# Scores of the first layer's attention: three products of upper and lower parts for head pairs 1 to 3

## The reference

```python
def _attend(q, k, v):
    s = jnp.einsum('bqkgd,bskd->bkgqs', q, k).astype(jnp.float32) * ATTN_SCALE
    p = jax.nn.softmax(s, axis=-1).astype(v.dtype)
    return jnp.einsum('bkgqs,bskd->bqkgd', p, v)

    o_lat = lax.map(lambda qb: _attend(qb, k_all, v_all), q_blocks)
    y_b = o_lat.swapaxes(0, 1).reshape(B_, S, B_WIDTH) * jax.nn.silu(bz)
```

## Time and profile before

| | |
|---|---|
| median of 3 runs | 1074.33 us (1074.14 to 1074.9) |
| profiled execution | 1075.35 us |
| its span in the trace | 1072.7 us |
| granted TensorE clock | 0.999 |
| PE busy | 1064.1 us (99%), 8092 matmuls |
| DVE busy | 721.6 us (67%) |
| ACT busy | 574.9 us (54%) |
| POOL busy | 141.2 us (13%) |
| first layer's attention, first scores to the last weighing | 193.3 to 267.7 us |

### The profile page before, as it was taken

How to read it: one execution, slowest core, us unless ns; L and a number is a source line. 1 busy time by engine, 2 the same in 40 slices (tenths; PEclk the granted TensorE clock), 3 DMA queues, 4 the chain that set the end, 5 groups by cost and what they waited for, 6 DMA issues and landing times.

```text
span 1072.7 us, 19921 instructions
## 1 busy us (share of the span) xinstructions
PE 1064.1 (99%) x8092; PEld 949.9 (89%) x8092; DVE 721.6 (67%) x1230; ACT 574.9 (54%) x977; POOL 141.2 (13%) x166
## 2 busy tenths in 40 slices
PE   9999999999999999999999999999999999999998
PEld 7887878656898999799999999999998799999997
DVE  5665566387554878778875676666677776766674
ACT  4532676544444567866565554444574555545454
POOL 0000010253200001632531000000023410000000
PEclk9999999999999999999999999999999999999999
DMA  9732121286613442057444364555543334555641
GB/s 382 319 137 66 75 79 40 93 289 213 232 41 119 141 145 80 6 193 236 148 168 158 119 236 161 194 186 170 198 155 103 134 119 153 202 201 177 211 178 39
DMA packets 25386, 168.77 MB, mean 157 GB/s; under 512 B 3280, under 2 KB 3536, under 8 KB 5456
## 3 DMA queue, kind: packets, MB, share of 16 engines
q1 hardware_dynamic: 25152, 167.25, 44.1%
q10 hardware_dynamic: 144, 0.26, 0.1%
HBM read 164.35 MB, written 1.05 MB: 154 GB/s over the span
## 4 chain that ended last, share of the span: by engine, by line
PE 96%; DVE 2%; ACT 2%; issue 0%; DVEq 0%; ACTq 0%
PE bank L437 26%; PE bank L438 25%; PE bank L439 25%; PE bank L1550 2%; PE bank L494 2%; PE bank L1714 2%; PE bank L1704 2%; PE bank L1694 1%; PE bank L1577 1%; PE bank L1568 1%; PE bank L446 1%; PE bank L2363 1%; PE bank L1395 1%; DVE wlo L415 1%; ACT TILE L1753 1%; PE bank L1688 1%
## 5 line engine op out<-in xcount | busy, mean ns | idle before, releaser
L437 PE MATMUL bank<-OPH,whi 128*128 128x256 f32 (+1 forms) x1716 | 519.7, 303 | 0.3
L439 PE MATMUL bank<-OPH,wlo 128*128 128x256 f32 (+1 forms) x1716 | 511.2, 298 | 0.0
L438 PE MATMUL bank<-OPL,whi 128*128 128x256 f32 (+1 forms) x1716 | 511.2, 298 | 0.0
L415 DVE TENSOR_TENSOR wlo<-raw,whi 128x1024 fp32r<-128x1024 f32 (+1 forms) x255 | 304.0, 1234 | 101.4 <-ACT whi L400 101.3
L437 PEld LDWEIGHTS bank<-OPH,whi 128*128 128x128 f32 x1716 | 328.0, 191 | 17.3 <-issue 5.2
L438 PEld LDWEIGHTS bank<-OPL,whi 128*128 128x128 f32 x1716 | 328.2, 191 | 10.0 <-issue 1.2
L439 PEld LDWEIGHTS bank<-OPH,wlo 128*128 128x128 f32 x1716 | 328.0, 191 | 9.8
L400 ACT ACTIVATE whi<-raw 128x1024 fp32r<-128x1024 f32 (+1 forms) x255 | 254.9, 1050 | 74.2 <-PE bank L439 71.9
L437 PE MATMUL bank<-whi,OPH 128*128 128x256 f32 (+2 forms) x272 | 93.8, 345 | 0.2 <-DVE OPL L717 0.2
L438 PE MATMUL bank<-wlo,OPH 128*128 128x256 f32 (+2 forms) x272 | 91.1, 335 | 0.0
L439 PE MATMUL bank<-whi,OPL 128*128 128x256 f32 (+2 forms) x272 | 91.1, 335 | 0.0
(11 more groups left out here) (291 smaller groups left out, 1132.6 us busy)
## 6 DMA issues: line engine op xcount, KB each, us to landing
raw<-in_stream SPq DMA_DIRECT2D x143, 1024.0 KB, 4.9
PROJ<-in_stream SPq DMA_DIRECT2D x5, 1024.0 KB, 18.4
raw<-in_stream SPq DMA_DIRECT2D x4, 1056.0 KB, 8.6
PROJ<-PROJ SPq DMA_DIRECT2D x32, 64.0 KB, 3.9
FIRST<-in_first SPq DMA_DIRECT2D x1, 1248.0 KB, 5.9
C<-in_con SPq DMA_DIRECT2D x1, 1157.5 KB, 7.2
FIRST<-in_first SPq DMA_DIRECT2D x1, 1024.0 KB, 8.0
WST<-in_w_s SPq DMA_DIRECT2D x2, 256.0 KB, 7.3
```

What stands on the lines that cost most here:

```text
L415: nc.vector.tensor_tensor(c.w[1][:, part], c.raw[:, part], c.w[0][:, part].bitcast(F32), ALU.subtract).then_inc(*raises(c.lo[h]))
L437: nc.tensor.matmul(out, w[0], x[0], start=start, stop=False, skip_group_check=skip)
L438: nc.tensor.matmul(out, w[0], x[1], start=False, stop=False, skip_group_check=skip)
L439: return nc.tensor.matmul(out, w[1], x[0], start=False, stop=stop, skip_group_check=skip)
```

## The change

- A new function `part_in_row` splits one 512-wide row into row `row` of OPH (ACT) and OPL (DVE), when its source is ready and the operand's last product (`pr.used`) is done.
- Behind step 2 both key rows of KDUP are split into rows 6 and 7. Behind steps 3, 6 and 10 the queries of pairs 1, 2 and 3 are split into rows 3, 4 and 5, which these pairs' outputs fill only later.
- The scores of pairs 1, 2 and 3 (blocks 4 to 15, six of the eight heads) are three products of these parts, the two heads in turn. Pair 0 keeps its plain products.
- The splits of output rows 6 and 7 move from steps 5 and 6 to steps 17 and 18, and wait for the last scores.

```diff
+            def part_in_row(self, row, src, before, free):
+                st = stage(f"qk{self.l}_row")
+                key = f"scores{self.l}"
+                def act(e):
+                    for point in due(e, before, free):
+                        e.wait_ge(*point)
+                    nc.scalar.activation(OPH[:, row, :], src, ACT.Copy).then_inc(*raises(("y_hi_made", key, row)))
+                def dve(e):
+                    for point in due(e, before, free, ("y_hi_made", key, row)):
+                        e.wait_ge(*point)
+                    nc.vector.tensor_tensor(OPL[:, row, :], src, OPH[:, row, :].bitcast(F32),
+                                            ALU.subtract).then_inc(*raises(("y_lo_made", key, row)))
+                st.act, st.dve = act, dve
+                return ("y_lo_made", key, row)
...
+                if p in self.apart:
+                    for point in due(e, self.apart[p]):
+                        e.wait_ge(*point)
+                    for n, (q, k) in enumerate(((OPH, OPH), (OPH, OPL), (OPL, OPH))):
+                        for r, h, rows in self.heads(j):
+                            mm = nc.tensor.matmul(self.S[j][r].mem[:, 0:nkb * P], q[rows, 2 + p, c0:c0 + P],
+                                                  k[rows, 6 + h // 4, kb0 * P:(kb0 + nkb) * P], start=n == 0, stop=n == 2)
                             if n == 2:
                                 mm.then_inc(*raises(self.S[j][r].full))
                     return
...
-                between = {0: lambda: job("co_0"), 1: lambda: job("co_1"), 2: mo.join_gates}
+                def query_part(p):
+                    at.apart[p] = [*key_parts, hn.part_in_row(2 + p, proj(QB + p)[:, 0, :], hn.q_ready[p], pr.used)]
+
+                def key_part(kv):
+                    key_parts.append(hn.part_in_row(6 + kv, KDUP[:, kv, :], hn.k_ready, pr.used))
+
+                key_parts = []
+                between = {0: lambda: job("co_0"), 1: lambda: job("co_1"),
+                           2: lambda: (mo.join_gates(), key_part(0), key_part(1)), 3: lambda: query_part(1),
+                           6: lambda: query_part(2), 10: lambda: query_part(3)}
...
-            split_at = {2: (0,), 3: (1,), 5: (6,), 6: (7,)} if l == 0 else {3: (0,), 4: (1,), 11: (6, 7)}
+            split_at = {2: (0,), 3: (1,), 17: (6,), 18: (7,)} if l == 0 else {3: (0,), 4: (1,), 11: (6, 7)}
...
+            if l == 0:
+                for k in (6, 7):
+                    y_keys[k] += [u.full for u in at.S[-1]]
```

More of the change, by code:

```diff
@@ L1660, in __init__ @@
                 self.S, self.E, self.T, self.O, self.full = [], [], [], [], []
+                self.apart = {}
             def take_step(self, j):
@@ L1689, in scores @@
                                                   k[rows, keys, SEQ:T], start=n == 0, stop=n == 2)
+                            if n == 2:
+                                mm.then_inc(*raises(self.S[j][r].full))
+                    return
+                if p in self.apart:
[5 more added lines that the diff above has]
+                                                  k[rows, 6 + h // 4, kb0 * P:(kb0 + nkb) * P], start=n == 0, stop=n == 2)
                             if n == 2:
```

## The result

The changed kernel takes 1078.97 us (median of 6, 1076.59 to 1079.7) against 1074.62 us before (median of 6): ratio 1.0038, 95% interval 1.0025 to 1.0051. It is 4.35 us slower, where 1.5 us were forecast; the time lies over the range. The profiled execution took 1079.7 us, with a span of 1077.9 us.

A forecast was written before the change was run, and what follows sets the result against it. PE's queue, busy 1064.1 of 1072.7 us, was taken as the bound: -1.38 (scores) - 0.12 (step 7) + 2.7 (scores of block 4) + 0.3 (row 5) = +1.5 us, median 1075.8 us, range 1073.1 to 1077.8 us.

The forecast's parts named there:

- The wait of block 4: Scores of block 4: PE waits 2.7 us for pair 1's lower query part, delayed through the DVE and ACT queues.
- The lower query part's surcharge: Pair 1's lower split on DVE beside POOL's gate multiplications: 0 to 0.84 us added to block 4's wait, 0.28 taken.
- The products: Scores of blocks 4 to 15 on PE: 0.90 us saved in six wide blocks, 0.48 in six narrow, 1.38 together.
- rival B: Narrow blocks: two heads' weight loads don't fit under 256 columns, each block takes 0.91 us; +3.7 us, 1078.0 us, chance 0.10.
- rows 5: Profile rows of PE's weight loads: one lasts 183 ns, a pair is busy 0.19 us together, read as loads running at once.
- Query parts of pairs 2 and 3 at nothing: Made behind steps 6 and 10, needed at 8 and 12: lateness covered, priced at nothing, else up to 0.56 us each.
- rival C: POOL holds up lower query parts, 0.56 us more at step 3, and blocks 8 and 12 wait: +3.2 us, 1077.5, chance 0.12.
- The 0.12 us before block 7: Scores of block 7: 0.12 us gained because the split of output row 6 leaves step 5.
- The moved splits at steps 17 and 18: End of attention: row 7's lower split delays row 5's, so PE waits 0.3 us there, bound 0 to 0.6 us.
- Rival A: Block 4's wait is hidden, DVE and ACT making the parts in their gaps: -1.2 us, 1073.1 us, chance 0.12.
- No other new wait above 0.5 us: Sign in the changed profile: besides block 4's wait of about 2.7 us, PE gets no new wait over 0.5 us.
- the 0.68 us row that the prediction counted against the exclusion: DVE split of 0.68 us, started while POOL worked; read as not showing that DVE with two SBUF inputs and POOL exclude each other.

The follow-up runs named there:

- experiment 1: Changed kernel with nine dummy float32 matmuls on PE ahead of block 4's wait for its parts: 1076.9 us, ratio 1.0019 to the kernel before.
- experiment 8: Changed kernel with POOL's two gate multiplications behind step 3 instead of 2, the DVE gates behind steps 5 and 6: 1077.98 us, ratio 1.0028 to before.
- experiment 6: Changed kernel with the parts spread over steps 1, 2, 5, 6 and 10, output splits at 7, 9, 11 and 17: 1074.7 us, ratio 1.0 to before.
- experiment 7: The kernel with spread parts (experiment 6), all parts made and waited for, but scores as plain float32 products: 1076.11 us.
- experiment 2: Changed kernel with all parts made and waited for, but scores of pairs 1 to 3 as plain float32 products: 1080.05 us.
- experiment 4: Changed kernel with output row 7 split at step 17 together with row 6, instead of step 18: 1078.62 us.
- experiment 5: Changed kernel with three products for pairs 2 and 3 only, key part behind step 5, row 6 split at 9, row 7 at 17: 1075.4 us, ratio 1.0006.
- experiment 3: Changed kernel with pair 1's query part made behind step 2, right after the key parts, instead of step 3: 1074.59 us, ratio 0.9997 to before.
- experiment 9: Changed kernel with key row 0 at step 1's end, key row 1 and pair 1's query behind 2, output splits at 9, 11, 13, 17: 1074.15 us, ratio 0.9994.
- experiment 10: Changed kernel with three products for pairs 2 and 3 only, key part behind step 2, output splits at 3, 9, 11, 17: 1073.23 us, ratio 0.9985.

## Why the prediction was wrong

**What bounds the kernel**, right: PE's queue. The waits of PE in this stage stand in the final time.

**The wait of block 4**, right in place and cause, near in size: 2.7 us forecast, 2.88 measured. The queues of ACT and DVE ran as followed. In the changed kernel's timelines of DVE (lower key parts, maxima of block 3, lower query part) and ACT (turned copy, upper query part):

```profile
212.16 1.31 DVE L1495 TENSOR_TENSOR OPL<-KDUP,OPH 128x512 fp32r<-128x512 f32 x2 [1.37 <-ACT OPH L1490]
...
214.29 0.75 DVE L1772 TENSOR_REDUCE STAT<-bank 128x1 f32<-128x256 f32 x2
...
216.80 1.34 DVE L1495 TENSOR_TENSOR OPL<-PROJ,OPH 128x512 fp32r<-128x512 f32 x1 [1.11 <-ACT OPH L1490]
...
215.65 0.60 ACT L1243 ACTIVATE TILE<-bank 128x512 f32<-128x512 f32 x1
216.13 0.64 ACT L1490 ACTIVATE OPH<-PROJ 128x512 fp32r<-128x512 f32 x1
```

The maxima come 1.9 us late against the trace of before with its offset of 0.2 us (2.16 forecast; the earlier trace rows). The lower query part's surcharge was 0.66 us, where I had taken 0.28 of a bound of 0 to 0.84. The two misses, 0.26 us too much and 0.38 us too little, nearly cancel, and that the size came out so near is partly luck.

**The step that failed** is the price of the wait: it stands in the sum as "2.7 (scores of block 4)", as if waiting cost PE what it lasts and nothing else. A stretch in which PE idles for 2.2 or 2.9 us has a second price, the low clock in what follows: 2.7 us in the profiled execution, about 2.1 us in the medians (1078.97 - 1076.9, experiment 1). I read the granted clock of the kernel before, 0.999 and a 9 in every slice (90% or more), and did not ask what kept it there: in that trace PE's longest wait is the 1.1 us for line 446 at the very start, which the changed kernel's list above has as well, and in this stage it waits 0.7 us in three pieces. The profile of before could not give the price, but a stretch of idling longer than any in it should have had a term of its own. There was a hint in the kernel itself: it already has a function `keep_clock` (line 441) that gives PE dummy matmuls of ones, called at lines 644 and 651, and experiment 1 uses it for the wait.

The Trainium skill ("TensorE: Matmul & The Clock Gate", Part 1: The HAM clock gate) says that an idle PE goes back to half rate. The traces agree, with 0.50 and 0.57 in the stretches behind an unfilled wait (the changed kernel, experiment 8) and 1.00 behind the filled one of experiment 1. The idle gaps that the page warns of are longer than the 2.9 and 2.2 us that were enough here; the measurement decides.

With that term the sum is 1.5 + 2.7 = 4.2 us, against the 4.45 us of the trace up to the end of the second layer. In the medians the clock is worth 2.1 us, and 3.6 of the 4.35 us are accounted for. Of the rest, experiment 1's trace has 0.4 us at the two late places.

**The products**, right in the price of a block and too high in the sum: 1.38 us forecast. The 1.41 us between the medians of experiments 6 and 7 look like a hit, but their traces have 1.02 us, and those of the changed kernel and experiment 2, the clock set aside, 1.14 us. A narrow block, in PE's timeline of the changed kernel, takes 232.65 - 232.09 = 0.56 us for the forecast 0.55, a wide one 0.89 to 0.91 at full clock:

```profile
232.09 0.39 PE L1718 MATMUL bank<-OPH 64*128 64x256 f32 x2
232.31 0.29 PE L1718 MATMUL bank<-OPL,OPH 64*128 64x256 f32 x2
232.43 0.29 PE L1718 MATMUL bank<-OPH,OPL 64*128 64x256 f32 x2
232.65 1.09 PE L1734 MATMUL bank<-FIRST,TILE 128*128 128x128 f32 x8
```

A product of 256 columns costs 0.12 us with its pair of loads, so rival B falls and rows 5 were read rightly. By the rule of the Trainium skill for loads ("TensorE: Matmul & The Clock Gate", section LDWEIGHTS) two in a row would be 0.21 us, an estimate from that page; the pair overlaps, and the measurement decides. What the prediction had wrong is that a shorter narrow block makes the next start earlier. In the changed kernel it does so only at blocks 11 and 15, 0.09 us each against experiment 2; at blocks 6, 7, 10 and 14 the next start comes when it came with the plain products. There the distances behind them grow by as much (the turning in step 6 takes 1.10 us to the next start, 228.87 to 229.97, and 1.02 us where nothing holds it); what holds it in each step I haven't followed. So the 0.48 us that stand in the sum for the six narrow blocks were at most 0.2.

**Query parts of pairs 2 and 3 at nothing**, right within 0.1 us: the profile shows no wait before blocks 8 and 12 of the changed kernel, and rival C falls as a whole, though its contention was there at step 3. **The 0.12 us before block 7**, too small: it is 3.97 us from block 6 to 7 before and 3.77 in the changed kernel and in experiment 2 alike, so none of these 0.20 us is the products'. The reading took the end of the eight weighing matmuls (0.66 us) for the distance to the next start, which is 0.59 us (231.50 to 232.09). Another 0.11 us come before block 8, in experiment 2 too. These 0.31 us for a forecast 0.12 nearly make up for what the narrow blocks didn't give, and that is luck. **The moved splits at steps 17 and 18**, right: 0.3 us, shown by experiment 4. Rival A fell with the wait. "No other new wait above 0.5 us" did not hold in the trace: the 0.60 us for DVE at 502.86 us are one, though not of the change.

**What stays open.** The 0.3 us at the end of the second layer, a wait for POOL, is there in the changed kernel and in experiments 1, 2, 4, 5 and 8. Experiments 3, 6, 7, 9 and 10 don't have it and even gain 0.25 us there on the kernel before, so two kernels with the same work there can lie 0.5 us apart. I haven't found what it hangs on. Experiment 9 is 0.5 us under before in the medians; its trace is 0.8 us ahead at block 15 against block 3, loses 0.5 us behind it and gains 0.25 us at the end of the second layer. Why its weight split on DVE stands in the way and that of experiment 10 doesn't, I haven't followed.

## What to carry to other kernels

Where an edit puts a wait on an engine that was never idle, price two things: the wait, and what its idling does to the clock of the work behind it. A few dummy matmuls into a bank that is free anyway are a cheap test for the second. In a sum of savings, ask also whether the next start is set by the bound engine at all: a narrow block that got 0.08 us shorter mostly passed nothing on. And when work is added to helper engines, follow each queue up to the next thing that the bound engine takes from it, in every step that gets a part: a part of 0.6 us that itself waits for another engine holds back whatever stands behind it, and in this kernel steps differ in what that is.

## What the runs showed of the hardware

PE's clock fell from 2.4 to 1.2 GHz within an idle stretch of 2.9 us in the changed kernel's trace and right behind one in experiment 2's, and behind one of 2.2 us in seven of ten executions of experiment 8 (by their mean clock and time), after more than 200 us of nearly unbroken work at full clock. In the changed kernel's trace it was low over the two stretches of 5.8 us that follow the wait, in experiment 8 for less. Behind the 1.2 us of experiment 3 it stayed, in all of 11 executions.

DVE's subtraction with both inputs in SBUF took 1.34 us beside POOL's multiplications and 0.69 us without them (experiment 8). An engine at 13% of the span lengthened PE's wait by 0.7 us. POOL pays too: its two gate multiplications took 2.95 us in the changed kernel, with that subtraction beside them, and 2.51 us in experiment 8 without:

```profile
216.33 2.95 POOL L2538 TENSOR_TENSOR PROJ<-PROJ 128x512 f32<-128x512 f32 x2
...
221.86 2.51 POOL L2538 TENSOR_TENSOR PROJ<-PROJ 128x512 f32<-128x512 f32 x2
```

That also answers the 0.68 us row that the prediction counted against the exclusion. It was POOL that lost time there: its normalisation beside that row took 2.56 us before, where the same two instructions without a DVE subtraction took 2.04 us in the changed kernel.
